# Last stage of a streaming encoder step: gates scaled inside the residual chain, two token tiles of r turned earlier, token sums asked for sooner, two additions moved to VectorE

## What is computed

```python
r = x + 0.5 * rms_norm(swiglu_ffn(rms_norm(x, norm_ffn1_pre), w_ffn1_gate_up, w_ffn1_down), norm_ffn1_post)
...
r = r + rms_norm(mixed, norm_mix_post)
r = r + 0.5 * rms_norm(swiglu_ffn(rms_norm(r, norm_ffn2_pre), w_ffn2_gate_up, w_ffn2_down), norm_ffn2_post)
gate = jax.nn.sigmoid(rms_norm(r, norm_ple_pre) @ w_ple_gate)
r = r + rms_norm(gate * (p @ w_ple_proj), norm_ple_post)
```

## Time and profile before

| what | us |
|---|---|
| median of 3 runs | 1086.64 |
| lowest and highest run | 1085.63, 1087.33 |
| the profiled execution, own time | 1087.3 |
| its span in the profile | 1085.5 |
| TensorE busy | 1041.0 (96%) |
| VectorE, ScalarE, GpSimd busy | 700.8, 510.5, 289.9 |

### The profile page before, as it was taken

How to read it: one execution, slowest core, us unless ns; L and a number is a source line. 1 busy time by engine, 2 the same in 40 slices (tenths; PEclk the granted TensorE clock), 3 DMA queues, 4 the chain that set the end, 5 groups by cost and what they waited for, 6 DMA issues and landing times.

```text
span 1085.5 us, 20075 instructions
## 1 busy us (share of the span) xinstructions
PE 1041.0 (96%) x8095; PEld 1015.4 (94%) x8095; DVE 700.8 (65%) x1057; ACT 510.5 (47%) x927; POOL 289.9 (27%) x222
## 2 busy tenths in 40 slices
PE   5999999999999999999999898999999999999896
PEld 4999999999999998887999798999999999999796
DVE  5998777776511269667694889777777651127843
ACT  4545555555522254434554544555555542126653
POOL 4113443431211132000323411434344021113311
PEclk8999999999999999999999999999999999999998
DMA  7222443425323313221222221333333532333002
GB/s 222 63 76 79 116 114 82 117 79 155 87 80 107 78 24 86 72 66 56 63 79 79 78 78 54 103 85 110 101 95 104 134 108 72 89 97 94 25 1 83
DMA packets 182678, 94.76 MB, mean 87 GB/s; under 512 B 11768, under 2 KB 180928, under 8 KB 182592
## 3 DMA queue, kind: packets, MB, share of 16 engines
q1 hardware_dynamic: 182576, 93.56, 31.1%
q10 hardware_dynamic: 16, 0.00, 0.0%
HBM read 91.15 MB, written 2.50 MB: 86 GB/s over the span
## 4 chain that ended last, share of the span: by engine, by line
PE 79%; DVE 14%; ACT 3%; issue 2%; POOL 1%; DMA 1%; DVEq 0%; SPq 0%; POOLq 0%; ACTq 0%
PE bank L1638 13%; PE bank L1640 13%; PE bank L1639 12%; PE bank L1748 9%; PE bank L1750 9%; PE bank L1751 9%; PE bank L1673 3%; PE misc L1802 2%; PE misc L1748 2%; PE misc L1750 2%; PE misc L1751 2%; DVE w_up L1072 1%; DVE x_lo L1102 1%; PE bank L1681 1%; DVE w_split L1072 1%
## 5 line engine op out<-in xcount | busy, mean ns | idle before, releaser
L1640 PE MATMUL bank<-h_hi,w_split 128*128 128x272 f32 x704 | 203.7, 289 | 0.0
L1638 PE MATMUL bank<-h_hi,w_split 128*128 128x272 f32 x704 | 203.0, 288 | 0.0
L1639 PE MATMUL bank<-h_lo,w_split 128*128 128x272 f32 x704 | 202.3, 287 | 0.0
L1072 DVE TENSOR_TENSOR w_split<-raw,w_split 128x1408 fp32r<-128x1408 f32 (+2 forms) x66 | 98.5, 1507 | 145.4 <-ACT w_split L638 145.4
L570 POOL TENSOR_TENSOR ssq<-ssq,sq 128x272 f32<-128x272 f32 x112 | 109.1, 974 | 238.7 <-ACT sq L643 228.0
L1639 PEld LDWEIGHTS bank<-h_lo,w_split 128*128 128x128 f32 x704 | 132.6, 188 | 0.1
L1638 PEld LDWEIGHTS bank<-h_hi,w_split 128*128 128x128 f32 x704 | 132.4, 188 | 0.1
L1748 PE MATMUL bank<-t_hi,even_blocks 128*128 128x272 f32 x432 | 126.0, 292 | 6.6 <-issue 3.7
L1640 PEld LDWEIGHTS bank<-h_hi,w_split 128*128 128x128 f32 x704 | 132.3, 188 | 0.0
L1750 PE MATMUL bank<-t_lo,even_blocks 128*128 128x272 f32 x432 | 125.6, 291 | 0.0
L1751 PE MATMUL bank<-t_hi,even_blocks 128*128 128x272 f32 x432 | 125.4, 290 | 0.0
(11 more groups left out here) (243 smaller groups left out, 2624.3 us busy)
## 6 DMA issues: line engine op xcount, KB each, us to landing
raw_up<-w_ffn_gate_up SPq DMA_DIRECT2D x88, 512.0 KB, 4.9
raw<-w_ffn_down SPq DMA_DIRECT2D x32, 704.0 KB, 4.8
raw<-w_in SPq DMA_DIRECT2D x14, 512.0 KB, 4.1
raw<-w_ple_gate SPq DMA_DIRECT2D x8, 512.0 KB, 3.8
x_tok<-x_prompt SPq DMA_DIRECT2D x4, 512.0 KB, 5.4
raw<-w_in SPq DMA_DIRECT2D x8, 256.0 KB, 3.8
raw<-w_out SPq DMA_DIRECT2D x16, 128.0 KB, 3.5
raw<-w_out SPq DMA_DIRECT2D x8, 256.0 KB, 4.0
```

The costliest lines, as they stand in the source:

```text
L1072: nc.vector.tensor_tensor(chunk_part(c, 1), chunk_raw(c), chunk_part(c, 0).bitcast(F32), ALU.subtract).then_inc(lo_made, 1)
L1638: nc.tensor.matmul(psum(u), wh, hi, start=(k == 0), stop=False)
L1639: nc.tensor.matmul(psum(u), wh, lo, start=False, stop=False)
L1640: mm = nc.tensor.matmul(psum(u), wl, hi, start=False, stop=(k == n - 1))
```

## The change

Six edits, all in or just ahead of the last stage:

1. VectorE's low part of the stage's fourth weight chunk (`split_lo(C0["ple"] + 3)`) moves from the end of the stage before to behind `ple_gate(0)`.
2. VectorE's `ple_gate(1)` moves into `chain_r(3, B)`, behind the update of block 5.
3. TensorE turns token tiles 0 and 1 of r (both in half A) ahead of the gates of g1 and g2, instead of inside g2 and behind its gates; those two now wait only for half A of r. ScalarE's `copy_r(0)` and `copy_r(1)` move accordingly, `copy_r(1)` to just ahead of the root of half B.
4. TensorE asks for the first token sums in the first gate unit of g6 at block 2, instead of in the second at block 6.
5. ScalarE takes `token_roots(0)` ahead of the sigmoids of g6.
6. The last two squares of all are added by VectorE instead of GpSimd.

```diff
@@ gpsimd
-                    run(SQ0["ple"] + 8 * g + 4 * h, h, 4, g == 0)
+                    run(SQ0["ple"] + 8 * g + 4 * h, h, 2 if (g, h) == (1, B) else 4, g == 0)
@@ scalar
             ple_gate(0)
+            copy_r(0)
             chain(3, B, SQ0["ple"] - KD)
             ple_square(0)
             ple_gate(1)
             ple_square(1)
+            copy_r(1)
             root(SUM0["down2"] + 3, D)
-            copy_r(0)
             for g in range(2, 2 * DOWN_GROUPS):
-                ple_gate(g)
                 if g == 6:
                     token_roots(0)
+                ple_gate(g)
...
-                if g <= XT:
+                if 3 <= g <= XT:
                     copy_r(g - 1)
@@ vector, last_group of the stage before
                 if with_p:
                     chain_lo(ci, A, range(KD // 2, KD))
                     p_lo(1), p_lo(2)
-                elif ci != 2:
+                    return
+                if ci != 2:
@@ vector
             ple_gate(0)
-            chain_r(3, B, y_down, SUM0["down2"] + 2, {2: lambda: ple_mul(0)})
-            ple_gate(1)
+            split_lo(C0["ple"] + 3)
+            chain_r(3, B, y_down, SUM0["down2"] + 2, {2: lambda: ple_mul(0), 5: lambda: ple_gate(1)})
             chain_lo(3, B)
             ple_mul(1)
             invert(SUM0["down2"] + 3, rpre[:, B, :])
+            def add_last(s):
+
+                dve.wait_ge(squared, s + 1 - KD)
+                dve.wait_ge(summed, s)
+                nc.vector.tensor_tensor(ssq[:, B, :], ssq[:, B, :], sq[:, s % 2, :], ALU.add).then_inc(summed, 1)
...
+            add_last(SUMMED[-1] - 2), add_last(SUMMED[-1] - 1)
             token_inverse(1)
@@ tensor, turn_r
-                pe.wait_ge(r_ready, 16 * 3)
+                pe.wait_ge(r_ready, 16 * 2 + KD if tt < 2 else 16 * 3)
@@ tensor, loop over g
+                if g in (1, 2):
+                    turn_r(g - 1)
                 if i == 0:
...
                     if h == B:
-                        turn_r(0)
                         all_sums(n2 + 3)
...
-                                {6: lambda: token_sums(0)} if g == 6 and m else None)
+                                {2: lambda: token_sums(0)} if g == 6 and m == 0 else None)
...
-                if 2 <= g <= XT:
+                if 3 <= g <= XT:
                     turn_r(g - 1)
```

More of the change, by code:

```diff
@@ L1325, in last_group @@
                     chain_lo(ci, A)
-                elif not with_p:
+                else:
                     chain_lo(ci, A, range(KD // 2, KD))
```

## The result

The changed kernel takes 1089.12 us (median of 6 runs, 1088.71 to 1090.78) against 1086.25 us (median of 6 runs, 1084.80 to 1087.33) of the kernel before on the same chip: ratio 1.0029, 95% interval 1.0019 to 1.0039, or 3.1 us slower (2.1 to 4.2). A second measurement beside 28 runs of the kernel before gave 1.0030 (1.0021 to 1.0040). The profiled execution took 1089.34 us, its span is 1087.6 us.

The account below looks back on a forecast made before the run. The prediction took VectorE's and ScalarE's chain through half B's root to bind up to g3, then TensorE. Terms +0.1, +2.2 and +0.1 summed to +2.4 us: 1089.7 for the profiled execution, 1089.0 against the median, range 1086.1 to 1090.8.

Parts of the forecast that it names:

- Bound of the stage: Last stage, 1003 to 1028.9: chain is VectorE, ScalarE's square, table and root, then VectorE; TensorE's first two idle times lie beside it.
- Weight split: Split moved behind the first gates: TensorE gets its bank 1.4 us sooner, nothing on the chain moves, 0.
- Gates of g1 inside the chain: Gates of g1 moved behind block 5: TensorE can start g2 at about 1016.3; 0 on the chain, bounds -0.5 to +1.0 us.
- Copy ahead of the root: ScalarE's copy of tile 1 ahead of half B's root: 1.02 us on the chain, g3 at 1030.05, +0.1 us.
- The clock behind g3's wait: Behind a new 4.6 us TensorE idle time ahead of g3: half clock costs +2.2 us, ends 0 and 3.4.
- Token sums: First sums in g6 asked for sooner, roots ahead of sigmoids: 1.8 us wait replaces 1.74 us, clock stays full, +0.1 us.
- Last two squares on VectorE: End of the last stage: TensorE's last sums did not wait for these additions, so 0.
- The clock costs nothing: Rival: low clock behind g3's idle time ends inside it or doesn't come; sum +0.2, 1086.8 us; chance 0.20.
- TensorE's idle time counts: Rival: half B's root doesn't bind, idle times ahead of g1, g2 and `turn_r(1)` shrink; -3.4 us, 1083.2; chance 0.08.
- Long low clock and bad meetings: Rival: 3.4 us of clock cost and two slow VectorE updates beside GpSimd; +4.6 us, 1091.2; chance 0.10.

Follow-up runs that it names:

- the kernel with the root moved: Changed kernel with ScalarE's root of half B right behind the sigmoids of g1 and token sums asked for where they were before: 0.9951 to the kernel before.
- filling: Changed kernel with 30 more matmuls, whose result nobody reads, in TensorE's idle time ahead of the gates of g3: 1.0025 to the kernel before.
- the early root and edit 5: Kernel before with the root of half B ahead of the squares of g1 and the token roots ahead of the sigmoids of g6: 0.9988 to the kernel before.

## Why the prediction was right, and where it was not

The forecast of 1089.0 us met 1089.12, and +2.4 us (for the profiled execution 1087.3 to 1089.7) met 1089.34 by the profile's own time. Part of that is luck: the stage lost 3.5 us, not 2.4.

*Bound of the stage: right.* The chain runs through VectorE and the root; TensorE's first two idle times lay in its shadow. Edits 1 and 2 alone gave 1.0007, and the kernel with the root moved showed the other side: with the root early, g3 comes 3.9 us sooner.

*Weight split, 0: right.* No idle time ahead of g1 and nothing gained from it.

*Gates of g1 inside the chain, 0 within -0.5 to +1.0: mis-sized.* It measured +0.4 us, a longer meeting with an addition of GpSimd, in eight profiles of nine. g2 started 13.28 us into the stage (1014.80 - 1001.52); my 1016.3 made it 13.3.

*Copy ahead of the root, +1.02 on ScalarE: right.* Behind the root it gave 0.92 us back. g3 was forecast 0.1 us later and came 0.33 later, by the meeting of the step above. The idle time was 4.10 us, not 4.6: TensorE was through 0.8 us later than I had it, waiting 0.44 us for a low part, and g3 came 0.3 us later.

*The clock behind g3's wait, +2.2 between 0 and 3.4: right in kind, too large in size.* It was the short stretch in every one of the five profiles with a wait of 3.2 to 4.1 us there, 3.4 us of half clock and 1.7 us of time (1.5 when measured by filling). I took a mean over three rows, of which the longest (3.1) was one that the same place had in some executions and not in others. The Trainium skill warns of long idle gaps ("TensorE: Matmul & The Clock Gate", "Why this matters for your kernels"), and these five waits of 3.19 to 4.11 us agree with it. The fall behind 1.73 us in g6 is not in that warning.

*Token sums, +0.1 with "1.8 us between full-speed matmuls leaves the clock alone, as 1.74 did": this is the step that failed.* The wait itself was 1.73 us, near the forecast 1.8, and the one ahead of `turn_y(1)` went. But the clock fell behind it in five profiles of six, and not behind the 1.74 us ahead of `turn_y(1)` in either of two. One row was no proof that an idle time of that length is free; the same prediction had a row where 1.97 us was not the earlier trace rows. Edits 4 and 5 together, +0.1 in the prediction, measured +1.6 us in the stage (77.73 against 76.18) and +1.2 by the ratio (1.0011). Against edit 5 alone, which would have sufficed, it is 3.5 us.

*Last two squares on VectorE, 0: right.* The pair takes 1.02 us instead of GpSimd's 1.66. From the last `y_gain` transposes to the token reciprocal it is 1.83 us (1079.39 to 1081.22) as before (1077.34 to 1079.18, 1.84). The Trainium skill ("GPSIMD Engine Reference", "Engine selection") has such an addition about twice as slow on GpSimd as on VectorE; here one took 0.76 us there before and 0.44 on VectorE now, 1.7 times, and the gain reached nobody.

*The rivals.* "The clock costs nothing" fell with the first stretch. "TensorE's idle time counts" fell in the changed kernel, and its condition, a root 3 us sooner, was the right one: with it, and the token sums late, the time fell by 0.5%. "Long low clock and bad meetings" had the right sum, 3.4 us of clock, from two short stretches in place of one long.

So the sum of the steps was 1.1 us short of what the stage lost: the clock at g3 taken 0.5 too large, g3 itself 0.2 too early, the clock in g6 left out, 1.7 (these terms are estimates from half the length of a stretch and leave 0.2 over). That 1089.34 was met all the same is owed to the 1.5 us that this execution got back before the stage, most of it at 677; and the medians differ by 2.9 us, from a median of before that was 0.4 us under the one I started from. Two misses of unlike sign met.

## What to carry to other kernels

Before work is put into an engine's idle time, ask whose shadow that idle time lies in, and move first what casts it: here one root, whose input had been ready for 4.7 us, stood behind squares and a copy that nobody waited for; moving it was worth 5 us in the stage, and made the rest of the change pay. Asking for a result sooner on an in-order engine only moves the wait, unless its producer is done by then. And idle time of TensorE can have a second price behind it, some 1.5 us here: look at the granted clock behind each wait, in more than one profile, and not at the sum of the waits. A wait behind which the clock stayed at full in one execution may lower it in the next.

## What the hardware showed

- The granted clock went to half for 3.4 us, in a few cases for 6.8. Behind waits of 3.19 to 4.11 us ahead of g3 it did so in five profiles of five. Behind 2.96 and 2.97 us ahead of g2 it fell in the kernel before and in the one with edits 4 and 5, not in the one with edit 5 alone and not in the one with the early root and edit 5; behind 2.37 us there it fell, behind 2.11 us and 1.46 to 1.49 us not.
- The same wait in the same place goes both ways from one execution to the next. Two waits lie far ahead of every edit: behind 1.97 to 1.98 us at 608 the clock fell in 9 of the 14 profiles, behind 3.48 to 3.50 us at 677 in 11 (for 6.8 us in four of them).
- Length alone doesn't decide: 1.73 us in g6, followed by four matmuls of one column (0.58 us for the four), fell in five of six; ahead of eight transposes 1.74 us did not in either of two, and neither did 2.32 us (edit 5 alone) or 2.53 us (edits 1 and 2) ahead of `turn_r(1)`. What makes the difference wasn't tried, and by the line above two profiles are few.
- Matmuls that nobody reads, put into the idle time, kept the clock at full in the one profile of that kernel (1.00 at 1029 in place of 0.50 at 1029 to 1032).
- The clock goes with much of the scatter: of 79 runs of the kernel before, the 22 with a mean granted clock of 0.995 took 1084.4 us on average, the 21 with 0.988 took 1086.8.
- VectorE's residual update took 0.49 us with no addition of GpSimd beside it, and up to 0.98 and 1.09 us when one was running or started with it (1014.81 and 1012.68 in the kernel before); 0.7 us of other work put ahead of two of them changed the pair from 1.05 to 1.47 us.
